# RWKV scan: the transposed factor made on VectorE, the walk spread in thirds over the growth of the inverses, the state's decay laid into the factor turns

## The reference, cut to what matters

```python
state, ys = lax.scan(_wkv_step, state0, scan_in)   # per token, per head
# S = S * decay_t + (S @ (-kk_t)) (kk_t * a_t)^T + v_t k_t^T ;  y_t = S r_t
```

## Time and profile before

| | |
|---|---|
| median of 3 runs | 5113.23 us (5110.92 to 5117.01) |
| the profiled execution | 5125.56 us, span 5123.7 us |
| busy in the whole span | PE 76%, PEld 54%, DVE 42%, ACT 26%, POOL 25% |
| mean granted TensorE clock | 0.861 |
| scan_R x Z, off x T, R turned by identity (matmul busy) | 154.8, 158.1, 148.5 us |

### The profile page before, as it was taken

How to read it: one execution, slowest core, us unless ns; L and a number is a source line. 1 busy time by engine, 2 the same in 40 slices (tenths; PEclk the granted TensorE clock), 3 DMA queues, 4 the chain that set the end, 5 groups by cost and what they waited for, 6 DMA issues and landing times. The chain is left out here.

```text
span 5123.7 us, 88817 instructions
## 1 busy us (share of the span) xinstructions
PE 3902.0 (76%) x34726; PEld 2768.3 (54%) x34726; DVE 2154.9 (42%) x4494; ACT 1353.8 (26%) x2725; POOL 1262.5 (25%) x918
## 2 busy tenths in 40 slices
PE   7765698776769879978677773876999998268774
PEld 6544576644557667856322222653888888232221
DVE  3433665445566543466100005642666664530002
ACT  3222331222233232221111101114555453111111
POOL 4101343320124334454100001321323332320000
PEclk9756899885889989989698886988999998679897
DMA  3211453222235322122699993334222221559997
GB/s 119 71 43 64 142 180 115 67 68 72 82 122 180 125 70 72 64 90 94 280 422 421 422 421 145 119 120 151 54 47 52 59 46 28 174 226 422 421 421 290
DMA packets 352692, 843.08 MB, mean 165 GB/s; under 512 B 128517, under 2 KB 191830, under 8 KB 292470
## 3 DMA queue, kind: packets, MB, share of 16 engines
q1 hardware_dynamic: 343822, 809.81, 43.8%
q0 software_dynamic: 8560, 28.85, 1.5%
HBM read 745.63 MB, written 92.93 MB: 164 GB/s over the span
## 5 line engine op out<-in xcount | busy, mean ns | idle before, releaser
L1139 DVE SCALAR_TENSOR_TENSOR f_ada<-first_hT,condition,f_ada 128x256 f32 (+1 forms) x672 | 287.0, 498 | 0.0
L2716 DVE TENSOR_TENSOR scan_R<-scan_R,scan_bank 128x256 f32<-128x256 f32 x240 | 100.8, 420 | 233.6 <-PE scan_bank L2739 231.8
L2000 PE MATMUL moe0e_p_g<-moe_ring,moe0e_xT 128*64 128x512 f32 x608 | 175.2, 657 | 18.1 <-ACT moe0e_xT L2038 9.7
L2490 POOL TENSOR_TENSOR scan_off<-scan_pairs,scan_join 128x256 f32<-128x256 f32 x240 | 174.2, 764 | 0.0
L343 POOL TENSOR_TENSOR gmi_w_lo<-gmi_w,gmi_w_hi 128x512 fp32r<-128x512 f32 x64 | 122.2, 1910 | 196.4 <-ACT gmi_w_hi L374 196.4
L2000 PE MATMUL moe0e_p_u<-moe_ring,moe0e_xT 128*64 128x512 f32 x608 | 167.9, 631 | 0.0
L2739 PE MATMUL scan_bank<-scan_T,scan_off 64*64 64x64 f32 x3840 | 158.1, 220 | 7.0 <-issue 1.9
L2739 PE MATMUL scan_bank<-scan_R,scan_Z 64*64 64x64 f32 x3840 | 154.8, 219 | 10.8 <-DVE scan_R L2716 9.9
L2000 PE MATMUL moe1e_p_g<-moe_ring,moe1e_xT 128*64 128x512 f32 x512 | 146.0, 650 | 15.2 <-issue 8.3
L343 POOL TENSOR_TENSOR p_w_lo<-p_w,p_w_hi 128x512 fp32r<-128x512 f32 (+3 forms) x88 | 112.8, 1283 | 176.1 <-ACT p_w_hi L374 176.1
L1100 POOL TENSOR_TENSOR f1u_w_lo<-f1u_w,f1u_w_hi 128x1024 fp32r<-128x1024 f32 x44 | 108.2, 2481 | 192.0 <-ACT f1u_w_hi L1109 192.0
(11 more groups left out here) (709 smaller groups left out, 10669.4 us busy)
## 6 DMA issues: line engine op xcount, KB each, us to landing
moe_ring<-in_moe_w_gu_dram SPq DMA_DIRECT2D x280, 1024.0 KB, 20.9
moe_ring<-in_moe_w_down_dram SPq DMA_DIRECT2D x140, 1024.0 KB, 22.4
first_hT<-in_ada_w_dram SPq DMA_DIRECT2D x48, 1024.0 KB, 7.3
f0u_w<-in_ffn_w_gate_up_dram SPq DMA_DIRECT2D x22, 1024.0 KB, 5.0
f1u_w<-in_ffn_w_gate_up_dram SPq DMA_DIRECT2D x22, 1024.0 KB, 4.9
gmi_w<-in_ga_w_in_dram SPq DMA_DIRECT2D x64, 256.0 KB, 2.7
p_w<-in_ab_w_in_dram SPq DMA_DIRECT2D x48, 256.0 KB, 2.6
f0d_w<-in_ffn_w_down_dram SPq DMA_DIRECT2D x44, 256.0 KB, 2.6
```

The lines of the kernel that those rows point to most:

```text
L1139: ins = nc.vector.scalar_tensor_tensor(out=dst, in0=src, scalar=cond[:, k, which:which + 1], in1=dst, op0=ALU.mult, op1=ALU.add)
L2000: mm = nc.tensor.matmul(p[r, :], xT[:, kd, r], ring[:, s, half, k, g * HID:(g + 1) * HID], start=(kd == 0), stop=(kd == KD - 1), skip_grou ...
L2490: nc.gpsimd.tensor_tensor(off[n][:], strict(u, g), over4(join[:, l + 1, :]), ALU.mult).then_inc(s["off_ready"], 1)
L2716: V.tensor_tensor(R[u][:, g4, :], R[u][:, g4, :], quad(zr_bank), ALU.add).then_inc(s["zr_added"], 1)
```

## The change

1. **T on VectorE.** The root turns (12 mmuls a head) and the grown turns (48) go, with their banks and ScalarE's 15 copies. VectorE writes T itself, by a transpose of 32x32 blocks of the 128x256 tile, after each identity add and after each R add of slots 0 to 11 (R has nothing outside of its 32x32 diagonal blocks that is needed there). It waits for its own add first.
2. **The walk in thirds.** The parts of steps 3 to 11 are placed one by one in the half slots of the growth (26 parts in 31 places); the products of y move from `walk_state` to `walk_solve`.
3. **The state's decay in the factor turns.** `bh` and `kh` are turned against a diagonal matrix `eed` (identity x ee, made by GpSimd, 128x704) instead of the identity; 11 chunks instead of 12, copied in three ScalarE copies instead of six. The state is then Sm = Sm x ee + ds in one VectorE operation; See is gone. at_rt and ee have three buffers.
4. **Factor work in halves** (the cumulative sum in quarters), placed in half slots.
5. **Signs as a column.** A 128x4 table gives each partition its sign, so that the exponentials run over all partitions (three instead of six); for it VectorE makes H1 and H2 instead of G2. t1 moves to ScalarE.
6. The copies of y move to ScalarE. There are two zr banks, so R x Z of slot n waits for the add of slot n-2. The bonus sums move from the body's start to behind the factor turns. sg is loaded first, by itself.

```diff
-    WALK_GROWTH = {n: NG + n for n in range(STEPS - NG)}
+    LATE = [(1, NG), (2, NG)] + [(what, j) for j in range(NG + 1, STEPS) for what in range(3)]
+    WALK_PARTS = {-1 + i * 2 * NZ // len(LATE): part for i, part in enumerate(LATE)}
+    WALK_PARTS[2 * NZ - 1] = (0, STEPS)
...
# GpSimd, end of factors(h)
+                    pool.wait_ge(s["bd_ready"], h + 1)
+                    nc.gpsimd.tensor_tensor(eed[:], eye[:]...broadcast_to([P, STEPS - 1, CH]),
+                                            ee[h % 3][:, 0:STEPS - 1]...broadcast_to([P, STEPS - 1, CH]), ALU.mult).then_inc(s["eed_made"], 1)
...
# ScalarE, exponentials and t1
-                        exps((e_exc, lo, G2, 1.0))
-                        exps((e_exc, hi, G, -1.0))
-                        exps((e_neg, lo, G, -1.0))
-                        exps((e_neg, hi, G2, 1.0))
-                        exps((e_inc, lo, G, 1.0))
-                        exps((e_inc, hi, G2, -1.0))
+                        A(t1[:], aa[:], ACT.Identity, scale=cols(h, 1), bias=oneminus[:, h:h + 1]).then_inc(s["t1_made"], 1)
+                        A(e_exc[:], H1[:], ACT.Exp).then_inc(s["exp_ready"], 1)
+                        A(e_neg[:], H2[:], ACT.Exp, scale=-1.0).then_inc(s["exp_ready"], 1)
+                        A(e_inc[:], H2[:], ACT.Exp).then_inc(s["exp_ready"], 1)
...
# VectorE, state, turn, growth
-                        V.scalar_tensor_tensor(out=Sm[:], in0=ds_psum, scalar=ee[w % 2][:, j:j + 1], in1=See[:], op0=ALU.mult, op1=ALU.add)
-                        V.tensor_scalar(See[:], Sm[:], ee[w % 2][:, j + 1:j + 2], None, ALU.mult)
+                        V.scalar_tensor_tensor(out=Sm[:], in0=Sm[:], scalar=ee[w % 3][:, j:j + 1], in1=ds_psum, op0=ALU.mult, op1=ALU.add)
...
+                    def turn(g):
+                        g4 = slice(4 * g, 4 * g + 4)
+                        V.transpose(T[:, g4, :]..., R[u][:, g4, :]...).then_inc(s["t_made"], 1)
...
+                        walk_part(2 * n)
+                        factor_part(fc, ahead, 2 * n)
                         dve.wait_ge(s["zr_ready"], h * NZ + n + 1)
-                        V.tensor_tensor(R[u][:, g4, :], R[u][:, g4, :], quad(zr_bank), ALU.add).then_inc(s["zr_added"], 1)
+                        V.tensor_tensor(R[u][:, g4, :], R[u][:, g4, :], quad(zr_bank[n % 2]), ALU.add).then_inc(s["zr_added"], 1)
+                        if l < LEVELS - 1:
+                            dve.wait_ge(s["zr_added"], h * NZ + n + 1)
+                            turn(g)
+                        walk_part(2 * n + 1)
+                        factor_part(fc, ahead, 2 * n + 1)
...
# TensorE
-                    turn_root(0)
-                    turn_root(1)
-                    turn_root(2)
...
-                        if 1 <= n <= NZ - NG:
-                            turn_grown(n - 1)
                         pe.wait_ge(s["z_copied"], h * NZ + n + 1)
-                        if n >= 1:
-                            pe.wait_ge(s["zr_added"], h * NZ + n)
+                        if n >= 2:
+                            pe.wait_ge(s["zr_added"], h * NZ + n - 1)
...
-                    pe.wait_ge(s["zr_added"], h * NZ + NZ)
...
# SyncE: sg by itself and first, then the other six
+                        sp.wait_ge(s["lw_ready"], h + 1)
+                        load_sg(ahead)
                         sp.wait_ge(s["bd_ready"], h + 1)
                         sp.wait_ge(s["kh_made"], h + 1)
                         load(ahead)
```

More of the change, by code:

```diff
@@ L2419, in _ @@
             def _(sp):
-                for dst, src in ((masks, a["rw_masks"]), (join, a["rw_join"]), (eye, a["rw_eye"]), (keep, a["rw_keep"]),
+                for dst, src in ((masks, a["rw_masks"]), (join, a["rw_join"]), (eye, a["rw_eye"]), (keep, a["rw_keep"]), (sides, a["rw_sides"]),
                                  (cols_all, a["rw_cols"].rearrange("h p c -> p h c"))):
@@ L2507, in walk_sa, with walk_part @@
                     A(SA[:], sa_psum, ACT.Identity, scale=w[w_ % 3][:, j:j + 1]).then_inc(s["sa_copied"], 1)
-                def exps(*of):
-                    for dst, rows, src, sign in of:
-                        A(dst[rows, :], src[rows, :], ACT.Exp, scale=sign).then_inc(s["exp_ready"], 1)
+                def walk_part(w, p):
+                    if w is not None and p in WALK_PARTS:
+                        what, j = WALK_PARTS[p]
+                        if what < 2:
+                            (walk_x, walk_sa)[what](w, j)
@@ L2686, in step, with walk_part @@
                             walk_step(walk, j)
+                    def walk_part(p):
+                        if walk is not None and p in WALK_PARTS and WALK_PARTS[p][0] == 2:
+                            walk_step(walk, WALK_PARTS[p][1])
                     mask(0)
@@ L2788, in part, with walk_part, bonus @@
                             what(walk, j)
-                    pe.wait_ge(s["bd_ready"], h + 1)
-                    pe.wait_ge(s["kh_made"], h + 1)
-                    if h:
-                        pe.wait_ge(s["bon_read"], h)
-                    for n in range(lat):
-                        mm = mmul(bon_psum[:, n:n + 1], rk[:, n, :], S.ones[:, 0:1])
-                    mm.then_inc(s["bon_ready"], 1)
+                    def walk_part(p):
+                        if walk is not None and p in WALK_PARTS:
+                            what, j = WALK_PARTS[p]
+                            if j < STEPS:
+                                (walk_state, walk_solve, walk_share)[what](walk, j)
+                    def bonus():
+                        pe.wait_ge(s["bd_ready"], h + 1)
+                        if h:
+                            pe.wait_ge(s["bon_read"], h)
+                        if h >= 2:
+                            pe.wait_ge(s["y_copied"], (h - 1) * lat)
+                        for n in range(lat):
+                            mm = mmul(bon_psum[:, n:n + 1], rk[:, n, :], S.ones[:, 0:1])
+                        mm.then_inc(s["bon_ready"], 1)
+                    pe.wait_ge(s["at_ready"], h + 1)
+                    pe.wait_ge(s["kh_made"], h + 1)
                     def pair_set(i):
@@ L2841, in body @@
                     part(walk_share, 2)
+                    turn(2)
+                    part(walk_state, NG)
                     pe.wait_ge(s["pb_masked"], h * NP + NP)
[L2843 to L2846 removed]
                     def grow_z(n):
@@ L2896, in _ @@
                         what(LAST, j)
-FACTOR_STEPS = 8
+FACTOR_STEPS = 12
 def rwkv_tables():
@@ L2916, in rwkv_tables @@
         joins.append(halves(b, b.T))
+    one, none = np.ones(CH, f), np.zeros(CH, f)
+    sides = np.stack([halves(LOG_DECAY * one, -LOG_DECAY * one), halves(-one, none), halves(none, -one), halves(0.5 * one, -0.5 * one)], 1)
     keep = np.ones((P, ALL), f)
@@ L2919, in rwkv_tables @@
     return {"rw_masks": np.ascontiguousarray(np.stack([strict, incl, strict, incl], 1)),
-            "rw_join": np.ascontiguousarray(np.stack(joins, 1)), "rw_keep": keep, "rw_eye": halves(same, same)}
+            "rw_join": np.ascontiguousarray(np.stack(joins, 1)), "rw_keep": keep, "rw_eye": halves(same, same),
+            "rw_sides": np.ascontiguousarray(sides)}
 def rwkv_join(nc, name, S, a, yS, bS, gate, out):
```

329 lines of the change are left out of this document (172 added, 157 removed).

## The result

The changed kernel takes 5028.28 us (median of 4 runs, 5024.05 to 5042.41), the kernel before 5115.12 in the same session (4 runs): a ratio of 0.9822 [0.9807, 0.9838], 87 us less. The profiled executions have spans of 5025.3 and 5123.7 us, 98.4 less, at mean clocks of 0.858 and 0.861.

What follows compares the result with a forecast made beforehand. TensorE's program order was taken as the bound (93% busy). Head part 11.9, growth 28.0 and loads 0.4 made 40.3 us a head against 48.68; 131 off 5125.6 gave 4994.6, median 4982; band 4950 to 5010 (0.55), range 4930 to 5060.

Steps and rivals of the forecast that it cites:

- the growth: Rest of each head after the head part: from 35.93 us to 28.0, 1.87 a slot.
- rival B: VectorE becomes the only bound: transposes at 0.63, blocking 1.0 more, 44.5 us a head, 5048 us; chance 0.17.
- rival C: Slower: TensorE's short waits bring the lower clock level, mean near 0.8, 5229 us; chance 0.08, including a transpose over 1.0.
- The 1.7 for the second zr bank: Growth slots 12 to 14 and the body's end: two banks and no last wait take 1.7 us off.
- the head part: From a body's start to its first growth product: from 12.75 us to 11.9.
- the loads' 0.4: Store and loads in one row on SyncE after the body's end: just fits, 0.4 us a head added, ends 0 and 1.5.
- Blocking, +1.0 a head, ends 0 and 2.5: VectorE's sum: one to three blocks by GpSimd of up to 0.58 more, less the See that goes.
- t1 to ScalarE: VectorE's sum a head: t1 leaves it, -0.7 us.
- The wait for `walk_state(2)`: Head part: VectorE's step 1 stands behind mask 4, scale 2, an identity add and a transpose, so it is late: +0.4.
- -5.6 for 48 turns: Growth: TensorE's 48 turns go, taking 5.6 us off a head.
- A: Rival, better cover: transposes at 0.3, waits from 7.1 to 4.3, 37.5 us a head, 4941 us; chance 0.17.
- D: Rival, does not pay: late loads and walk step, slots lock to the slower engine, 47.5 to 49.5 a head; chance 0.03.

Runs made afterwards that it cites:

- km_late: The changed kernel with one wait more: GpSimd's km waits until both H tiles are made; 5004.99 us, 0.9774 of the kernel before.
- km_four: The changed kernel with km at its old place beside G, in four instructions of 192 columns; 5013.66 us, 0.9773 of the kernel before.
- late_whole: The changed kernel with km waiting for both H tiles and the factor work in whole pieces; 4997.26 us, 0.9748 of the kernel before.
- zero_early: The changed kernel with km waiting for both H tiles and Sm cleared ahead of the last R add; 4998.94 us, 0.9748 of the kernel before.
- best: The changed kernel with km behind the H tiles, whole factor pieces and Sm cleared before the last R add; 4999.33 us, 0.976 of the kernel before.
- whole: The changed kernel with factor work in whole pieces again (cumulative sum in two halves); 5023.76 us, 0.9813 of the kernel before.
- t_alone: The kernel before with only T moved to VectorE's transposes, no turns on TensorE; 5111.01 us, 0.9983 of the kernel before.
- state_first: The kernel before with T on VectorE alone, and Sm made ahead of the R add and transpose; 5064.61 us, 0.9878 of the kernel before.
- turn_twice: The changed kernel with every transpose made twice, the first into a spare tile; 5094.09 us, 0.9943 of the kernel before.

## Why the prediction was right or wrong

**Right: direction, range, and most of the sizes outside the growth.** The time, 5028, lies inside the whole range (4930 to 5060) but above the forecast's own band of 4950 to 5010, between it and rival B's 5048. By its own steps: transposes 0.445 for 0.42, and never stretched (445 to 448 over 240, though `off` products run beside many of them); VectorE 33.8 us a head for 33.4 (79% busy, just under the 80% named as a sign); TensorE's records less by 3471; the last walk 30.4 as before; no wait on a load in the bodies; clock 0.97 in the 14 heads, so rival C did not come, though its mechanism did in small, six more pieces at the lower level at up to 1.5 us, some 0.6 a head. Head 15 gave 8.6 (44.0 to 4227.06 - 4191.66 = 35.4) for 7, the start of the scan 6.0 for 3, since lw starts 8.7 us after the stage's first DMA issue where it started 13.5 after, and the bonus sums left that stretch. Head 0 gave -0.3 for 3: the turns go and the lower level is granted for longer, 0.82 against 0.94. Together 14.3 for 13. Of the remaining 3.8 of the 98.4, 3.5 are earlier stages, since the scan itself starts that much sooner (3526.93 for 3530.41).

**Wrong: 40.3 us a head measured 42.94**, so 80.3 us in place of 118. All of the shortfall is there. A little of it is arithmetic: the growth's terms, 35.93 - 5.6 - 0.35 - 1.7, make 28.3 and not 28.0, so the sum is 40.6 a head and 4987 us. (By the same sum 39 to 42.5 a head are 4965 to 5014 us, not 4950 to 5010, and VectorE's terms add up to 33.5.) The 1.7 for the second zr bank came from no row; before, TensorE waits for the R add 15.9 us in these 14 heads, 1.1 a head. By its steps: the head part 12.5 (3847.00 to 3859.48) for 11.9, the growth 30.4 for 28.4 with the loads' 0.4.

*The term "Blocking, +1.0 a head, ends 0 and 2.5".* It named the mechanism and its rule, and took its blocks from `off` products and eed (at most 0.58 each), operations whose place the prediction had looked up. It did not ask where km goes when t1 leaves VectorE: the edit "t1 to ScalarE" was booked as -0.7 on VectorE and no more. km is the longest instruction GpSimd has in the growth, 1.93 us, and it came to stand beside G. Measured: km_late takes 20 us of 14 heads off VectorE, 1.4 a head, nearly all of it in G; together with the pieces at the lower level that are fewer it was worth 2.1 us a head by km_late, 1.8 by km_four. The counts of pieces go with km's place (ten, 15 and 13 where it stands whole beside G; three, one, two, one and five in km_late, km_four, late_whole, zero_early and best), but how the block brings them on is not shown: whole has 13 with no wait over 1.3 us, and before, four came without the block. The blocks beside `off` products, where the prediction did look, are there too: the quarters of the cumulative sum average 0.784 for 0.56 alone, 0.9 a head, the same with km late. Together 2.3 a head of blocks, inside the ends given; and VectorE's sum was right to 0.4. The price lay not in the sum but in the place, right ahead of an R add, a transpose and Sm. eed, priced at 1.7, took 1.365.

*The head part.* The zero of the state is made by VectorE at the body's start and TensorE waits 0.73 for it; the prediction had no term for that. zero_early has 0.46 less a head, about 0.3 of it by heads without a piece. Without these two the kernel stands at 40.37 in zero_early, near the 40.3 of the forecast and under its corrected 40.6. How near is partly luck: one piece at the lower level fell into that execution, and the next paragraph shows that the sum's largest term had the wrong reason. The wait for `walk_state(2)` was foreseen (+0.4): before, TensorE waited 0.3 each for steps 1 and 2, now 1.07 for step 2 alone.

*But the sum was right for a reason partly wrong.* "-5.6 for 48 turns" rests on the first part's sentence that the stage "is bound by TensorE's program order, with small waits in it". t_alone refutes it as the whole story: a growth slot is also one turn of the recurrence X, SA, increment, Sm. Taking 0.47 of issue out of the slot and laying a transpose of 0.45 into the recurrence left it at 2.62; with the R add and the transpose behind Sm it is 2.14 to 2.3. The turns pay only if the recurrence is loosened too, by the walk in thirds (which the prediction priced at next to nothing by itself) or by Sm ahead of the add (state_first). The missing step was to time the recurrence in the slot from the same rows and to compare it with the slot; the range held because both parts of the change came together.

**The rivals.** B ended nearest in time (5048, 44.5 a head), but not by its mechanism: transposes were not 0.63, and VectorE is busy 79%. It is right in this much, that each of the two engines waits for the other and added work on VectorE shows (turn_twice). A needed transposes at 0.3; its 37.5 was reached by no version. D's 47.5 to 49.5 holds what part 1 gave alone, 47.90.

What stays open: what brings a piece at the lower level on, and so how many a version will have; why whole pieces bring nothing although VectorE's sum falls with them (74% busy in best, 80% in zero_early); and what the slots of the best versions wait for now, with TensorE at 90%. One wait is known: the 1.07 us in `walk_state(2)` stands in every head of all of them.

## What to carry to other kernels

Before work taken off the busiest engine is priced, the recurrence that runs through the same slot must be timed: 93% busy says that the engine is nearly full, not that nothing else is as long. When an operation moves to an engine that is free earlier, its consumers move too; look up what each of them comes to stand beside, above all a long GpSimd instruction beside a VectorE one with two SBUF inputs, and delay it or cut it in four. On an in-order engine, put what the recurrence waits for ahead of bulk work that is ready at the same time: one moved line was worth 3.3 us of 47.9 here, 1.9 of it without the clock. And where the granted clock changes in pieces, compare heads without a piece before a few tenths are put down to an edit.

## What the runs showed of the hardware

VectorE's transpose of 128x256 fp32 from SBUF to SBUF takes 445 to 448 ns in all 240 instances, `off` products on GpSimd beside many of them, and 402 ns where it follows directly on another one (turn_twice). A VectorE operation with two SBUF inputs beside one GpSimd instruction of 1.9 us went from 0.55 to as much as 2.12 us; with that instruction in four parts the mean of both halves fell from 1.22 to 0.67 although GpSimd took half as long again. The granted clock went to its lower level for pieces of 3.5 to 14 us inside heads that otherwise run at the upper one: ten in the kernel after, with waits of 2.6 to 3.0 us in it, six of the ten near the end of such a wait, and 15 in another execution of the same kernel; three in km_late and one in km_four, where the longest wait is 1.6 and 1.8 us; 13 in whole, where it is 1.3; four in the kernel before, where none is over 0.84. A piece of 3.5 us cost up to 1.5 us. Half of the long waits had none near them, and what decides was not isolated.
